# Feed-forward: gated values turned in 32x32 squares on VectorE and put in place by small SBUF DMAs instead of transposes on TensorE

## What is computed

```python
def hybrid_layer(x, ...):
    ...                                     # attention half, not touched
    h = rms_norm(x, g_ffn_pre)
    f = jax.nn.silu(h @ w_gate) * (h @ w_up)        # (256, 2816)
    x = x + rms_norm(f @ w_down, g_ffn_post)
    return x
```

## Time and profile before

| | |
|---|---|
| median of 3 runs | 598.49 us |
| the profiled execution, its own time | 598.48 us |
| its span, first to last instruction | 596.7 us |
| TensorE matmuls (PE) | 585.4 us busy, 98% |
| VectorE (DVE) | 362.0 us busy, 61% |
| ScalarE (ACT) | 292.8 us busy, 49% |
| GpSimd (POOL) | 42.1 us busy, 7% |
| DMA queue of the loads | 105.73 MB, 48.9% of 16 engines |
| granted TensorE clock | 0.998 of full speed |

### The profile page before, as it was taken

The page is one execution under the profiler, slowest core; times in us unless marked ns, Lnnn a source line. Parts: engine busy times, 40 slices in busy tenths (PEclk is TensorE's granted clock), DMA queues, the critical chain, the costliest instruction groups (busy, mean ns, idle before and its releaser), DMA issues.

```text
span 596.7 us, 7657 instructions
## 1 busy us (share of the span) xinstructions
PE 585.4 (98%) x3004; PEld 486.1 (81%) x3004; DVE 362.0 (61%) x469; ACT 292.8 (49%) x417; POOL 42.1 (7%) x68
## 2 busy tenths in 40 slices
PE   7999999999999999999999999999999999999996
PEld 4878887888888889888888888788888888898884
DVE  4888965947536546165497987567645536533632
ACT  6574663755453444153446745665554453424420
POOL 1100001410000000000120100034000000000000
PEclk9999999999999999999999999999999999999999
DMA  8872632437655541559266343507565555342701
GB/s 313 328 239 104 230 142 107 168 125 284 235 168 186 210 154 59 211 224 331 80 239 212 142 159 122 196 6 278 194 244 172 200 171 186 137 184 99 281 1 70
DMA packets 18291, 107.26 MB, mean 180 GB/s; under 512 B 2768, under 2 KB 3024, under 8 KB 6608
## 3 DMA queue, kind: packets, MB, share of 16 engines
q1 hardware_dynamic: 17968, 105.73, 48.9%
q10 hardware_dynamic: 288, 1.05, 0.5%
HBM read 105.72 MB, written 1.05 MB: 179 GB/s over the span
## 4 chain that ended last, share of the span: by engine, by line
PE 85%; DVE 6%; ACT 6%; DMA 1%; issue 1%; DVEq 0%; POOLq 0%; POOL 0%; ACTq 0%
PE bank L1083 75%; PE bank L1123 4%; ACT work L559 3%; DVE w_l L729 3%; PE bank L1173 2%; DVE bank L835 2%; PE bank L1108 2%; ACT w_h L494 2%; PE bank L1148 1%; DMA work<-in_x_first_transposed 1%; DVE actT_l L756 1%; DVE top L835 0%; ACT actT_h L521 0%; ACT work L575 0%; DVE neg_max L839 0%
## 5 line engine op out<-in xcount | busy, mean ns | idle before, releaser
L729 DVE TENSOR_TENSOR w_l<-raw,w_h 128x2048 fp32r<-128x2048 f32 x91 | 207.7, 2290 | 144.2 <-ACT w_h L494 144.1
L494 ACT ACTIVATE w_h<-raw 128x2048 fp32r<-128x2048 f32 x91 | 173.9, 1917 | 143.0 <-PE bank L1083 118.1
L1083 PE MATMUL bank<-w_h,actT_h 128*128 128x512 f32 (+1 forms) x600 | 232.3, 387 | 0.2
L1083 PE MATMUL bank<-w_h,actT_l 128*128 128x512 f32 (+1 forms) x600 | 225.9, 377 | 0.0
L1083 PE MATMUL bank<-w_l,actT_h 128*128 128x512 f32 (+1 forms) x600 | 225.2, 375 | 0.0
L1083 PEld LDWEIGHTS bank<-w_h,actT_h 128*128 128x128 f32 x600 | 113.1, 189 | 22.6 <-issue 2.7
L1083 PEld LDWEIGHTS bank<-w_h,actT_l 128*128 128x128 f32 x600 | 112.9, 188 | 21.2
L1083 PEld LDWEIGHTS bank<-w_l,actT_h 128*128 128x128 f32 x600 | 113.2, 189 | 18.3
L1083 PE MATMUL bank<-w_h,fT_h 128*128 128x512 f32 x160 | 49.8, 392 | 0.0
L1083 PE MATMUL bank<-w_h,fT_l 128*128 128x512 f32 x160 | 49.3, 389 | 0.0
L1083 PE MATMUL bank<-w_l,fT_h 128*128 128x512 f32 x160 | 49.3, 389 | 0.0
(11 more groups left out here) (73 smaller groups left out, 377.0 us busy)
## 6 DMA issues: line engine op xcount, KB each, us to landing
raw<-in_w_blocks SPq DMA_DIRECT2D x91, 1024.0 KB, 4.9
bias<-in_b_in SPq DMA_DIRECT2D x8, 256.0 KB, 6.3
raw<-in_w_blocks SPq DMA_DIRECT2D x2, 512.0 KB, 7.0
x<-in_x SPq DMA_DIRECT2D x2, 512.0 KB, 14.1
gain_b<-in_g_attn_post SPq DMA_DIRECT2D x2, 512.0 KB, 8.2
bias<-in_g_ffn_pre SPq DMA_DIRECT2D x2, 512.0 KB, 5.6
gain_b<-in_g_ffn_post SPq DMA_DIRECT2D x2, 512.0 KB, 5.6
work<-in_x_first_transposed ACTq DMA_DIRECT2D x1, 516.0 KB, 6.2
```

What stands on the lines that cost most here:

```text
L494: nc.scalar.activation(w["h"][:, slot(b), :], raw[:, r, :], ACT.Copy).then_inc(hi_ready, 1)
L729: nc.vector.tensor_tensor(w["l"][:, slot(b), :], raw[:, slot(b, RAW), :], w["h"][:, slot(b), :].bitcast(F32), ALU.subtract).then_inc(lo_re ...
L1083: ins = nc.tensor.matmul(bank[BANK_OF[name]][:, 0:n], left[s][:, at + k, tokens(t)], right[r][:, k, c * BANK:c * BANK + n], start=first an ...
```

## The change

The transposes of `f` on TensorE are gone, with their banks. In their place:

- `squares_f` (DVE, L965 of the changed kernel) transposes each 32 x 32 square of `f[t]` within its 32 partitions and writes the squares of one target quadrant side by side into `squares[t]`.
- `exchange` (SP, L364) moves them between the four partition quadrants: 16 DMAs for each (c, t), each 32 partitions x 128 floats (64 floats for c = 5), from `squares[t]` to `crossed[t]`. They are issued in two halves of 8, behind the weight loads of blocks 13 + 4c + 9 to 13 + 4c + 12: first t = 0 in two halves, then t = 1. The first half of each t waits for `squares_ready[t]`, and for `f_lo_ready` of the chunk before.
- `hi_f` (ACT, L567) and `lo_f` (DVE, L972) make `fT_h` and `fT_l` from `crossed[t]` in SBUF where `hiT` and `loT` made them from the bank.
- `hi_f` and `lo_f` of chunks 0 to 3 stand in the next chunk, behind `after(L, b + 2)`. Those of chunk 4 stand behind `after(L, 36)`, with `squares_f` of chunk 5 behind them on DVE; those of chunk 5 stand behind `after(L, 40)`. TensorE waits for chunk 3's before block 35 and for chunk 5's before block 42 (`f_landed`).

```diff
+            def exchange(L, c, t, half):
+                if half == 0:
+                    place_free(squares_ready[t], f_count(L, c))
+                    if L or c:
+                        place_free(f_lo_ready, F_PARTS.before(L, (c, t)) - 1)
+                n = 32 * f_blocks(c)
+                for i in (2 * half, 2 * half + 1):
+                    for j in range(4):
+                        sp.dma_start(work[32 * j:32 * j + 32, 4 + t, i * n:(i + 1) * n],
+                                     work[32 * i:32 * i + 32, 2 + t, j * n:(j + 1) * n]).then_inc(crossed_in[t], 16)
...
@@ SP, behind each load_block(L, b)
+                    for c in range(FFN_CHUNKS):
+                        after_swiglu = b - (FIRST_FFN + 4 * c + 9)
+                        if 0 <= after_swiglu < 4:
+                            exchange(L, c, after_swiglu // 2, after_swiglu % 2)
...
@@ ACT
+            def hi_f(L, c, t):
+                act.wait_ge(crossed_in[t], 256 * f_count(L, c))
+                nc.scalar.activation(f_part("h", c, t), f_view(c, t), ACT.Copy).then_inc(f_hi_ready, 1)
...
                 for c in range(1, FFN_CHUNKS):
                     b = FIRST_FFN + 4 * c
-                    hiT(L, ("ft", c - 1, 0))
                     after(L, b)
-                    hiT(L, ("ft", c - 1, 1))
                     silus(L, c, 0)
                     silus(L, c, 1)
-                    for q in range(1, 2 if c == FFN_CHUNKS - 1 else 4):
-                        after(L, b + q)
-                hiT(L, ("ft", FFN_CHUNKS - 1, 0))
-                after(L, FIRST_DOWN)
-                hiT(L, ("ft", FFN_CHUNKS - 1, 1))
-                for b in range(FIRST_DOWN + 1, NB - 4):
+                    after(L, b + 1)
+                    if c < FFN_CHUNKS - 1:
+                        after(L, b + 2)
+                        hi_f(L, c - 1, 0)
+                        hi_f(L, c - 1, 1)
+                        after(L, b + 3)
+                for b in range(FIRST_DOWN, NB - 4):
                     after(L, b)
+                    for c, at in ((FFN_CHUNKS - 2, 1), (FFN_CHUNKS - 1, 5)):
+                        if b == FIRST_DOWN + at:
+                            hi_f(L, c, 0)
+                            hi_f(L, c, 1)
...
@@ DVE
+            def squares_f(L, c, t):
+                b = BANK_OF["up", c, t]
+                n = P * f_blocks(c)
+                dve.wait_ge(drained[b], HELD[b].done(L, ("up", c, t)) + 1)
+                if L or c:
+                    dve.wait_ge(crossed_in[t], 256 * (f_count(L, c) - 1))
+                nc.vector.transpose(squares[t][:, 0:n].rearrange("p (j k b) -> p j k b", j=4, b=32),
+                                    f[t][:, 0:n].rearrange("p (k j b) -> p j k b", j=4, b=32)
+                                    ).then_inc(squares_ready[t], 1)
...
@@ TensorE
                 for c in range(1, FFN_CHUNKS):
                     b = FIRST_FFN + 4 * c
-                    multiply(L, 0, b)
-                    f_transposed(L, c - 1, 0)
-                    multiply(L, 1, b)
-                    f_transposed(L, c - 1, 1)
-                    for q in range(1, 2 if c == FFN_CHUNKS - 1 else 4):
+                    for q in range(2 if c == FFN_CHUNKS - 1 else 4):
                         multiply(L, 0, b + q)
                         multiply(L, 1, b + q)
...
+                f_landed(L, FFN_CHUNKS - 3)
                 for b in range(FIRST_DOWN, NB - 4):
                     multiply(L, 0, b)
-                    if b == FIRST_DOWN:
-                        f_transposed(L, FFN_CHUNKS - 1, 0)
                     multiply(L, 1, b)
-                    if b == FIRST_DOWN:
-                        f_transposed(L, FFN_CHUNKS - 1, 1)
...
+                f_landed(L, FFN_CHUNKS - 1)
                 for b in range(NB - 4, NB):
                     multiply(L, 0, b)
```

More of the change, by code:

```diff
@@ L195, in trunk @@
         f = [work[:, 8 + t, :] for t in range(T)]
+        squares = [work[:, 2 + t, :] for t in range(T)]
+        crossed = [work[:, 4 + t, :] for t in range(T)]
         v = {MOBA: sb("v_moba", [P, T, GROUP]), SWA: sb("v_swa", [P, T, KV])}
@@ L260, in trunk @@
         half_ready = sem("half_ready")
+        squares_ready = [sem(f"squares_ready{t}") for t in range(T)]
+        crossed_in = [sem(f"crossed_in{t}") for t in range(T)]
+        f_hi_ready = sem("f_hi_ready")
+        f_lo_ready = sem("f_lo_ready")
         pool_step = sem("pool_step")
@@ L285, in trunk @@
                      ("mix", SWA, 1), ("mix", MOBA, 0), ("mix", MOBA, 1), ("ht", 1, 0, 0), ("ht", 1, 0, 1),
-                     ("ht", 1, 1, 0), ("ht", 1, 1, 1)] + [("ft", c, t) for c in range(FFN_CHUNKS) for t in range(T)])
+                     ("ht", 1, 1, 0), ("ht", 1, 1, 1)])
+        F_PARTS = Order([(c, t) for c in range(FFN_CHUNKS) for t in range(T)])
         def transposed(name):
@@ L1000, in _ @@
                 after(L, 15)
+                squares_f(L, 0, 0)
                 swiglu(L, 0, 1)
                 after(L, 16)
+                squares_f(L, 0, 1)
                 for c in range(1, FFN_CHUNKS):
@@ L1005, in _ @@
                     end = b + (1 if c == FFN_CHUNKS - 1 else 3)
-                    loT(L, ("ft", c - 1, 0))
                     after(L, b)
-                    loT(L, ("ft", c - 1, 1))
                     for q in range(b + 1, end):
                         after(L, q)
+                    if c < FFN_CHUNKS - 1:
+                        lo_f(L, c - 1, 0)
+                        lo_f(L, c - 1, 1)
                     swiglu(L, c, 0)
                     swiglu(L, c, 1)
+                    if c < FFN_CHUNKS - 1:
+                        squares_f(L, c, 0)
                     after(L, end)
-                loT(L, ("ft", FFN_CHUNKS - 1, 0))
-                after(L, FIRST_DOWN)
-                loT(L, ("ft", FFN_CHUNKS - 1, 1))
-                for b in range(FIRST_DOWN + 1, NB - 4):
+                    if c < FFN_CHUNKS - 1:
+                        squares_f(L, c, 1)
+                for b in range(FIRST_DOWN, NB - 4):
                     after(L, b)
+                    for c, at in ((FFN_CHUNKS - 2, 1), (FFN_CHUNKS - 1, 5)):
+                        if b == FIRST_DOWN + at:
+                            lo_f(L, c, 0)
+                            lo_f(L, c, 1)
+                    if b == FIRST_DOWN + 1:
+                        squares_f(L, FFN_CHUNKS - 1, 0)
+                        squares_f(L, FFN_CHUNKS - 1, 1)
                 scale_y(L, 1, 0)
@@ L1183, in mix, with f_landed @@
                 transpose(L, ("mix", g, t), lambda q: o[t][:, q * P:(q + 1) * P], 4)
-            def f_transposed(L, c, t):
-                b = BANK_OF["up", c, t]
-                pe.wait_ge(drained[b], HELD[b].done(L, ("up", c, t)) + 1)
-                transpose(L, ("ft", c, t), lambda q: f[t][:, q * P:(q + 1) * P], min(4, KF - 4 * c))
+            def f_landed(L, c):
+                pe.wait_ge(f_lo_ready, F_PARTS.done(L, (c, T - 1)))
             def rows_landed(L, ph, t):
```

23 lines of the change are left out of this document (15 added, 8 removed).

## The result

| | median us | runs | span us | granted clock |
|---|---|---|---|---|
| before | 598.5 | 598.32 to 598.55 | 596.7 | 0.998 |
| after | 667.3 | 666.45 to 667.93 | 666.1 | 0.95 |

The change makes the kernel slower: ratio 1.115, interval 1.113 to 1.117. The forecast was 600.9 in a range of 595.9 to 608.5. Slower is right, by 29 times the amount that was forecast (68.8 us against 2.4).

What follows compares the result with a forecast made beforehand. TensorE, busy 98% of the span, was taken as the bound. 598.48 us less 10.6 for transposes, plus 5.0 and 4.0 at block 39 and twice 2.0 at block 42, gave 600.9 us, range 595.9 to 608.5.

Steps and rivals of the forecast that it cites:

- The transposes, 10.6 us: Feed-forward on TensorE: removing the transpose groups of both layers saves 10.6 us.
- The step on SP: SP's queue: small DMAs start 0.44 us apart (0.37 to 0.55), so a load and its 8 take 4.05 us.
- the 0.67 of the third row: SP's queue: the third DMA row's own time, 0.67 us; the upper step of 0.55 was set midway to it.
- the threshold of 0.59: SP's queue: at 0.59 us or more a small DMA, every round is longer than a block's 5.44 us.
- SP becomes the bound: Rival, feed-forward loads: 610 us at steps of 0.55, near 620 at 0.67; chance 0.11 for steps of 0.5 or more.
- In chunks 1 to 4 it is hidden: Chunks 1 to 4: SP's 4.05 us rounds fit under a block's 5.44 us, so the squares DMAs cost nothing.
- three blocks of cover: Chunks 1 to 4: slots freed four blocks ahead leave the next low part three blocks, 16 us, of cover.
- the wait of swiglu on squares_ready: DVE: swiglu's wait is met by DVE's own earlier work; no cost was put in the sum.
- Blocks 39 and 42: TensorE stalls: 5.0 and 4.0 us at block 39 in the two layers, 2.0 us a layer at block 42.
- the landing with the load: Block 39, lower bound: squares land together with load 41, 4.8 us after issue, giving a stall of 3.6 us.
- The clock: Rival: waits at block 39 bring the 1.2 GHz level, 606 us; price four times if at block 42 too; chance 0.12.
- their fixed cost overlaps: Squares DMAs: the fixed cost of about 2 us does not come once for each; otherwise a round takes over 16 us.

Runs made afterwards that it cites:

- Run 6: Changed kernel with both token tiles in one squares DMA, 16 a chunk behind two loads, and chunk 5's hi_f and lo_f one block earlier: 588.1 us, ratio 0.983.
- run 1: Kernel before, transposes kept, plus 8 small DMAs with unused results behind each weight load of the feed-forward: 602.75 us.
- Run 7: Changed kernel with both token tiles in one squares DMA, and chunk 4's last quarter behind load 40 instead of 41: 601.9 us, ratio 1.006.
- run 11: Changed kernel with unread matmuls added on TensorE, 9 ahead of block 34, 5 ahead of block 39 and 5 ahead of 42: 666.1 us, ratio 1.113.
- run 8: Changed kernel with both token tiles in one squares DMA, all issued by GpSimd, and chunk 5's hi_f and lo_f one block earlier: 589.7 us, ratio 0.986.
- run 3: Changed kernel with its 384 squares DMAs issued by GpSimd instead of SP, same sizes and waits: 591.2 us, ratio 0.989.

## Why the prediction was wrong

**The transposes, 10.6 us: right.** Run 6 is 10.3 us under the kernel before.

**The step on SP: the term that was mis-sized.** I took 0.44 us from start to start, with 0.37 and 0.55 as ends, from DMAs whose source is HBM. It measured 0.63. The rows held no DMA from SBUF to SBUF, and I noted only that none had 32 partitions, which run 1 shows not to matter, and not the source, which does. The honest upper bound was the 0.67 of the third row; I had it and went only half the way to it. A round became 5.6 instead of 4.05 us, on the far side of the threshold of 0.59 which the rival "SP becomes the bound" named.

**"In chunks 1 to 4 it is hidden": the step that failed.** The prediction gave the reason that "even if ACT waits there for 1 or 2 us, the next low part has three blocks of cover", and that "the wait of swiglu on squares_ready is met by DVE's own earlier work". ACT waited up to 11.8 us at this copy, 103.7 us in all with chunk 4's, and TensorE stood 34.5 us for swiglu. Each wait was looked at alone. The wait itself is met, but swiglu stands in DVE's order behind lo_f, which waits for ACT, which waits for the DMAs, which wait for squares_f, which stands behind the swiglu before. I counted three blocks of cover for the low parts and did not look at the banks. The ring was never added up: 4 x 5.6 for the rounds, 1.8 to 2.9 for the landing, 0.6 + 0.7 for the copies, 1.4 for two swiglu and 0.7 for squares_f are 27.6 to 28.7 us against 21.8 of matmuls. Even with my 0.44 it is 4 x 4.05 + 5.2 = 21.4 or more: nothing to spare. That slower came out right is owed to the mechanism only in part: of 57.8 us of waits, 23.3 stand at the two places of the forecast, and for the other 34.5 it had no term.

**The rival's price.** The rival "SP becomes the bound" named the right place and gave 620 at a step of 0.67, by letting the loads fall behind by 0.7 us a round. The loads were the wrong victim (run 1: 4 us). In the ring each turn loses some 6 us. Against run 6 the stretch from block 17 to block 35 is 22.6 us longer in the first layer and 21.8 in the second, and that from block 35 to the last block 17.5 and 16.9. So more than half of the loss against run 6 stands ahead of block 35, where the forecast had none.

**Blocks 39 and 42.** Forecast 5.0 and 4.0, and twice 2.0. Measured in the kernel after 6.0 and 6.1, and 5.8 and 5.3. Run 7 shows that the cause at block 39 is the one given. With 0.63 for the step the forecast's sum for block 39 gives 255.84 + 8 x 0.63 + 2.1 + 4.9 - 262.12 = 5.8, close to what was measured. For block 42 the same sum gives about 7.5 at 0.63; that its 5.7 for a step of 0.55 lies near the measured 5.8 is chance. Blocks 39 to 41 took 19.5 us instead of 16.3, part of them at the lower clock, and that ate some of the wait. These steps were right in kind. Two bounds were miscounted: at block 39 the rows give 3.4 for the landing with the load, not 3.6, and 5.1 for steps of 0.55, not 5.9.

**The clock.** That idle time of this length brings the lower clock was a rival with 0.12; it happened. PE's rows behind the wait at block 39 and the windows around the longest wait, PEclk the third column from the end:

```profile
286.65 1.22 PE L1157 MATMUL bank<-w_h,fT_h 128*128 128x512 f32 x2 [5.98 <-DVE w_l L776]
214.00:242.00 28.00, 22.80 (x122) 19.35 (x121) 12.70 (x10) 9.62 (x8) 0.00 (x0) 1.00 0.50 169
242.00:262.00 20.00, 11.02 (x63) 10.48 (x64) 8.48 (x9) 4.96 (x5) 0.00 (x0) 0.74 0.35 118
```

A pair of matmuls that took 0.62 us in the earlier trace rows takes 1.22 behind 6 us of idle time. The Trainium skill, "TensorE: Matmul & The Clock Gate", section Why this matters for your kernels, warns of such gaps. The trace agrees: the lower clock stands at nine of the ten waits, all but the one of 3.1 us in front of block 31. Whether this price comes on top of the wait depends on what ends the next wait. At block 39 it did (run 7, 4.7 us for two waits); where the ring ends the next wait, some 8 us of it cost nothing (run 11).

**squares_f** took 0.70 us for 512 columns, as assumed. The rule of "DMA: Bandwidth & Descriptors", section Rules for kernel authors, in the Trainium skill, to make many small transfers into few, I set aside because their fixed cost overlaps. It does (landings of 2.9 us at steps of 0.63; the first ones behind SP's pause, with nothing else in the queue, land 1.8 us after their issue). What does not overlap is the issue on SP, one DMA after another, and for that the rule held: half the DMAs brought back 52 us.

**What stays open:** why a DMA with its source in SBUF takes SP 0.64 us and one from HBM 0.46; how much of the 22 us at the lower clock the kernel after would get back; and why GpSimd's DRAIN takes 5.9 us behind its DMAs where it took 0.7.

## What to carry to other kernels

When a change puts a consumer's wait ahead of the work that feeds its producer, write down the whole ring and add up one turn of it against the time that the engine which sets the pace needs for the same work; cover looked up wait by wait does not show it. Price the issue of many small DMAs on the engine that issues them, from rows with the same source and target, before their bytes or their latency. And where a first version is slower, try fewer, wider transfers and earlier places before giving it up: the same idea is 1.7% faster than before here, with 16 DMAs a chunk instead of 32, two loads instead of four and one copy moved.

## What the runs showed of the hardware

- A DMA on SP's queue steps by 0.63 to 0.64 us when its source is in SBUF and by 0.46 to 0.47 when it is in HBM, both into SBUF, at 16 KB, for 32 or 128 partitions (run 1). GpSimd steps by 0.49 for the same SBUF to SBUF DMAs (run 3).
- Squares DMAs of 32 partitions x 512 bytes land 1.8 us behind their issue with nothing else in the queue, and 2.9 us (median) in the kernel after.
- A group of four pipelined 128 x 128 float32 transposes costs TensorE 0.48 us, 0.12 each, where one seems to take 0.27; VectorE's 32 x 32 transpose of 128 x 512 float32 took 0.70 us.
- The DRAIN at the end of GpSimd's program took 5.9 us in run 8 and 4.6 in run 3, where GpSimd issues the DMAs, and 0.7 in run 6, where it issues none.
- 1.22 us for a pair of matmuls behind 6 us of idle time, against 0.62: the clock had fallen from 2.4 to 1.2 GHz.
